# Second gate half moved into token block 1 and computed from an exponential, block sums moved behind two dots, second norm's rows in a buffer of their own

## The chip, the cores and the metric

The kernel runs on one core of a Trainium2 chip. The metric is the device time of one execution in microseconds (us). The version before takes 1873.3 us, the median of three runs (1871.72 to 1873.37).

## The reference, cut to what matters

Two decoder layers over 256 tokens of width 1024, float32. Each layer is a token mixer (attention, pooling, gated DeltaNet) with a first LayerNorm, and then the stage that this change touches:

```python
def peer_ffn(h, w_q, sub_k1, sub_k2, u_tab, v_tab):
    ...                      # 8 heads; per token and head the 16 best of 128*128 experts: idx, wts
    def block(args):         # two blocks of 128 tokens
        xb, ib, wb = args
        u_sel = u_tab[ib]
        act = jax.nn.gelu(jnp.einsum('thkd,td->thk', u_sel, xb), approximate=False)
        return jnp.einsum('thk,thkd->td', act * wb, v_tab[ib])
...
ffn = peer_ffn(h, peer_wq[i], peer_k1[i], peer_k2[i], peer_u[i], peer_v[i])
ple = jax.nn.sigmoid(h @ ple_gate[i]) * (p[i] @ ple_proj[i])
h = layer_norm(DEEPNORM_ALPHA * h + ffn + ple, ln2_g[i], ln2_b[i])
```

The `u` row and the `v` row of an expert lie side by side in HBM, 1024 floats each, so one expert is 8 KB.

## The kernel before, in words

**The stage of the experts.** Each layer treats its 256 tokens as two blocks of 128. Within a block, 8 heads times 16 ranks give 128 steps. Step n fetches for each of the 128 tokens its expert of that rank: an indirect DMA of 128 rows of 8 KB, 1 MB, issued by GpSimd (L680 in block 0, L698 in block 1) into slot n mod 8 of a ring of 8 slots. When it has landed, VectorE multiplies the first half with the tokens' rows of `h` and sums (the dot: L1722, in block 1 L1752). ScalarE makes the GELU, the weight and a 128x128 diagonal matrix of it (L1319 to L1323, in block 1 L1343 to L1349). TensorE multiplies the diagonal with the second half of the slot and adds into the PSUM tile `acc` (L912, in block 1 L931): two halves of 512 columns. Its end frees the slot (semaphore `row_used`), and GpSimd may issue the gather of step n+8.

**What stands between the steps.** `steps()` is a hand-written list of the order. VectorE chooses, in small pieces behind the dots, the experts of a later head (`select_head`). TensorE also makes the later heads' scores and, in block 0, the embedding's two products: `pp` (from the projection) and `pg` (the gate, `h @ ple_gate`), each for column halves c = 0, 1 and token blocks b = 0, 1. The gate's 4 MB of weights come in 8 pieces; `("pgw", c, j)` multiplies piece j of half c for both blocks, 8 matmuls (L799). `rows_later` lets ScalarE treat the finished gate one row later than TensorE, and VectorE two rows later. ScalarE applies the sigmoid (L1479), VectorE multiplies with the projection and adds alpha*h into `base` (L1957, L1958).

**Between the blocks.** `acc` holds one block's sum. Behind block 0's last dot VectorE waits for TensorE's last product, adds `acc` to `base` of block 0 (L1705), and TensorE then writes `base` of block 1 into `acc` by an identity product (L924) and goes on with block 1. Block 0 is unrolled in the program. In block 1 the first 6 (VectorE, ScalarE), 7 (TensorE) or 8 (GpSimd) heads are a loop on the chip.

**The norm's rows.** The gains and shifts of a LayerNorm, 1 MB when spread over the partitions, are loaded by GpSimd into `lnr`: for the first norm at L668, for the second at L671, when block 0 and 1 of the first norm are done; that is just ahead of the stage's first gather, on the same queue.

## Time and profile before

| | |
|---|---|
| median of 3 runs | 1873.3 us |
| profiled execution | 1873.84 us, span 1872.0 us |
| gathers (L680, L698) | 512, 536.9 MB of the 660.6 MB moved |
| TensorE busy | 1696.2 us, 91% |
| VectorE busy | 1371.0 us, 73% |
| ScalarE busy | 904.6 us, 48% |
| mean granted TensorE clock | 0.995 |

The span falls in four parts: the dense part of layer 0 (about 0 to 287 us), its experts (to about 931 us), and the same for layer 1 (to about 1215 and 1861 us), then the last norm and the output. Busy shares are averages over parts with different limits. In the slices of the page each place stands for 46.8 us.

### The profile page before, as it was taken

To read this page: it belongs to the slowest core of one execution; us is meant where nothing else is said; L and a number is where in the kernel's file an instruction comes from. 1 tells how busy PE (TensorE), PEld (TensorE's weight loads), DVE (VectorE), ACT (ScalarE), POOL (GpSimd) and SP (SyncE) were. 2 spreads that over 40 slices of the span, in tenths; PEclk is the share of its full clock that TensorE was granted. 3 is DMA by queue.
4 is the path that set the end of the run, shared out by engine and by line. 5 is a ranking of instruction groups with operands and counts; after the bars stand their busy time and mean duration, and the time that the engine had idled before them with its cause. 6 is when DMAs were issued, how large, how long until landed. Compare 5 with 4: busy or idle time off the path is not lost.

```text
span 1872.0 us, 26665 instructions
## 1 busy us (share of the span) xinstructions
PE 1696.2 (91%) x7454; PEld 976.1 (52%) x7454; DVE 1371.0 (73%) x3499; ACT 904.6 (48%) x2247; POOL 683.2 (36%) x585
## 2 busy tenths in 40 slices
PE   8999999999999787777799999999999998887876
PEld 8977886544444232222289778865443432222222
DVE  5987768877777777776568976787777777777754
ACT  5566534544445444444455674345444454444443
POOL 0110004544444455555311100045443555555553
PEclk9999999999999999999999999999999999999999
DMA  6644779999999999999955357799999999999997
GB/s 251 191 125 150 257 248 407 416 427 427 426 427 417 426 425 428 427 428 428 408 184 168 119 191 247 275 415 420 426 427 427 423 402 413 427 427 428 428 427 304
DMA packets 106730, 660.63 MB, mean 353 GB/s; under 512 B 11888, under 2 KB 12288, under 8 KB 40064
## 3 DMA queue, kind: packets, MB, share of 16 engines
q0 software_dynamic: 75376, 546.57, 69.8%
q1 hardware_dynamic: 31248, 112.74, 17.8%
q8 instruction: 54, 0.88, 0.2%
q14 instruction: 52, 0.43, 0.1%
HBM read 658.20 MB, written 1.06 MB: 352 GB/s over the span
## 4 chain that ended last, share of the span: by engine, by line
PE 53%; DMA 25%; issue 9%; DVE 6%; ACT 5%; POOL 1%; DVEq 1%; POOLq 0%; ACTq 0%
PE acc L912 14%; DMA arena<-experts_dram,stage 10%; DMA arena<-experts_dram,idxu 9%; PE psum L736 6%; PE psum L737 6%; PE psum L738 6%; DMA cst<-experts_dram,stage 5%; PE acc L931 4%; PE psum L767 4%; PE psum L799 2%; PE acc L736 2%; DVE arena L1722 1%; PE acc L738 1%; PE acc L737 1%; PE psum L826 1%
## 5 line engine op out<-in xcount | busy, mean ns | idle before, releaser
L931 PE MATMUL acc<-arena 128*128 128x512 f32 x896 | 440.2, 619 | 118.8 <-ACT arena L1349 118.5
L912 PE MATMUL acc<-arena 128*128 128x512 f32 x896 | 412.2, 601 | 23.9 <-ACT arena L1323 23.7
L1752 DVE CUSTOM_DVE_ANT_0 arena<-arena,h 128x1024 f32<-128x1024 f32 x224 | 274.9, 1227 | 140.8 <-DMA arena<-experts_dram,stage 60.1
L698 POOL DMA_INDIRECT arena<-experts_dram,stage x224 | 295.2, 1318 | 226.9 <-PE acc L931 173.4
L931 PEld LDWEIGHTS acc<-arena 128*128 128x128 f32 x896 | 156.9, 192 | 400.5 <-issue 400.3
L1722 DVE CUSTOM_DVE_ANT_0 arena<-arena,h 128x1024 f32<-128x1024 f32 x224 | 274.5, 1226 | 117.4 <-DMA arena<-experts_dram,idxu 113.8
L680 POOL DMA_INDIRECT arena<-experts_dram,idxu x224 | 247.6, 1105 | 300.3 <-PE acc L912 268.3
L912 PEld LDWEIGHTS acc<-arena 128*128 128x128 f32 x896 | 163.0, 189 | 251.5 <-issue 152.1
L1601 DVE TENSOR_TENSOR raw_r<-raw,w_hi_r 128x1024 fp32r<-128x1024 f32 x150 | 177.8, 1220 | 59.5 <-ACT w_hi_r L1229 58.6
L1343 ACT ACTIVATE gel<-dots 128x1 f32<-128x1 f32 x256 | 51.9, 203 | 294.5 <-DVE dots L1752 293.6
L1229 ACT ACTIVATE w_hi_r<-raw 128x1024 fp32r<-128x1024 f32 x152 | 154.2, 1054 | 50.9 <-DMA raw<-weights_dram 50.8
L1319 ACT ACTIVATE gel<-dots 128x1 f32<-128x1 f32 x256 | 51.3, 200 | 234.5 <-DVE dots L1722 233.6
L1349 ACT ACTIVATE arena<-cst,gw 128x128 f32<-128x128 f32 x256 | 102.8, 401 | 41.7 <-ACT gw L1346 16.9
L1323 ACT ACTIVATE arena<-cst,gw 128x128 f32<-128x128 f32 x256 | 102.8, 401 | 8.4
L736 PE MATMUL psum<-w_hi_r,hidden_r 128*128 128x512 f32 x256 | 101.2, 395 | 2.9 <-DVE raw_r L1601 1.9
L737 PE MATMUL psum<-raw_r,hidden_r 128*128 128x512 f32 x256 | 99.8, 390 | 0.0
L738 PE MATMUL psum<-w_hi_r,hidden_r 128*128 128x512 f32 x256 | 99.8, 390 | 0.0
L736 PE MATMUL psum<-hidden_r,w_hi_r 128*128 128x256 f32 x320 | 91.4, 286 | 0.0
L738 PE MATMUL psum<-hidden_r,raw_r 128*128 128x256 f32 x320 | 90.5, 283 | 0.0
L737 PE MATMUL psum<-hidden_r,w_hi_r 128*128 128x256 f32 x320 | 90.5, 283 | 0.0
L1346 ACT ACTIVATE gw<-gel,wst 128x1 f32<-128x1 f32 x256 | 75.4, 294 | 24.6 <-ACT gel L1343 1.7
L671 POOL DMA_DIRECT2D lnr<-lnrows_dram x2 | 1.1, 538 | 225.4 <-DVE h L1594 225.4
(294 smaller groups left out, 2702.6 us busy)
## 6 DMA issues: line engine op xcount, KB each, us to landing
raw<-weights_dram SPq DMA_DIRECT2D x168, 512.0 KB, 3.7
arena<-weights_dram SPq DMA_DIRECT2D x20, 512.0 KB, 4.6
w_hi<-weights_dram SPq DMA_DIRECT2D x12, 512.0 KB, 5.8
lnr<-lnrows_dram POOLq DMA_DIRECT2D x4, 1024.0 KB, 8.0
arena<-experts_dram,idxu POOLq DMA_INDIRECT x224, 13.2
arena<-experts_dram,stage POOLq DMA_INDIRECT x224, 13.7
lnr<-cum_dram POOLq DMA_DIRECT2D x2, 1024.0 KB, 9.1
cst<-weights_dram SPq DMA_DIRECT2D x4, 512.0 KB, 4.0
```

The lines of the kernel that those rows point to most:

```text
L680: nc.gpsimd.indirect_dma_start(slots[n % RING][:, :], None, experts[:, :], bass.IndirectOffsetOnAxis(idxu[:, n:n + 1], 0)).then_inc(slot_i ...
L698: nc.gpsimd.indirect_dma_start(slots[i % RING][:, :], None, experts[:, :], bass.IndirectOffsetOnAxis(stage[:, i:i + 1], 0)).then_inc(slot_ ...
L736: mm(dst, left[0], right[0], start=start, stop=False)
L737: mm(dst, left[0], right[1], start=False, stop=False)
L738: return mm(dst, left[1], right[0], start=False, stop=stop)
L912: last = mm(acc[:, c * 512:(c + 1) * 512], diag[:, i % 4, :], slots[n % RING][:, D + c * 512:D + (c + 1) * 512], start=n == 0, stop=n == R ...
L931: last = mm(acc[:, c * 512:(c + 1) * 512], diag[:, i % 4, :], slots[i % RING][:, D + c * 512:D + (c + 1) * 512], start=False, stop=ends)
L1229: AC(w_hi[:, n % HIS, :], raw[:, raw_slot(L, piece), :], ACT.Copy).then_inc(w_hi_ready, 1)
L1323: AC(diag[:, i % 4, :], ident, ACT.Copy, scale=gw[:, i:i + 1]).then_inc(diag_ready, 1)
L1601: TT(w_lo[:, s, :], raw[:, s, :], w_hi[:, n % HIS, :].bitcast(F32), ALU.subtract).then_inc(w_lo_ready, 1)
L1722: nc.vector.tensor_tensor_reduce(slot[:, 0:D], slot[:, 0:D], h[:, 0, :], 1.0, 0.0, ALU.mult, ALU.add, dots[:, i:i + 1]).then_inc(dot_ready, 1)
L1752: nc.vector.tensor_tensor_reduce(slots[i % RING][:, 0:D], slots[i % RING][:, 0:D], h[:, b, :], 1.0, 0.0, ALU.mult, ALU.add, dots[:, i:i + ...
```

## The change

The diff has six edits.

- The gate's half c = 1 leaves block 0: its weight pieces are multiplied by TensorE behind four steps of block 1 (`GATE_AT`: head 0 steps 4 and 10, head 1 steps 0 and 6), ScalarE drains it behind head 1 step 12, VectorE finishes it behind head 1 step 14. Half 0's four pieces stand further apart, and are finished at head 7.
- The sigmoid is made in two parts: ScalarE writes exp(-x), and VectorE adds 1 and takes the reciprocal (`gate_in`).
- Block 0's sums (`block_sums`) stand behind the second dot of block 1. Their upper half goes to `first_sums`, a free piece of `hidden`, until the gate's upper half is done. TensorE writes only the lower half of `base` of block 1 ahead of block 1's products, and the upper half at head 7.
- The first two heads of block 1 are unrolled on TensorE, ScalarE and VectorE (`OPENING = 2`).
- The second norm's rows go to `lnr2`, loaded in the dense part, behind the loads of `cdiag` and `ckeys`.
- GpSimd's descriptor scratch is 8192 bytes of a partition where the default is 16384, which makes room for `lnr2`.

```diff
-    beside |= {at: [("pgw", 0, j)] for j, at in enumerate(((5, 7), (5, 12), (5, 15), (6, 4)))}
-    beside |= {at: [("pgw", 1, j)] for j, at in enumerate(((6, 6), (6, 9), (6, 12), (7, 4)))}
-    beside |= {(6 + c, 5): [("pg", c, 0), ("pg", c, 1)] for c in range(2)}
+    beside |= {at: [("pgw", 0, j)] for j, at in enumerate(((5, 7), (5, 13), (6, 5), (6, 11)))}
+    beside |= {(7, 11): [("pg", 0, 0), ("pg", 0, 1)]}
...
+OPENING = 2
+GATE_AT = ((0, 4), (0, 10), (1, 0), (1, 6))
+GATE_OUT, GATE_IN = 12, 14
...
                         pool.dma_start(ckeys, every.broadcast_to([P, FH, T])).then_inc(ckeys_in, 16)
+                        pool.dma_start(lnr2[:, :], lnrows[L, 1]).then_inc(ln2_in, 16)
...
-                    if step == ("select", 0):
-                        pool.wait_ge(h1_ready, NB * (L + 1))
-                        pool.dma_start(lnr[:, :], lnrows[L, 1]).then_inc(ln_in, 16)
...
-                        pe.wait_ge(base_ready, L * NB + 2)
-                        for c in range(2):
-                            mm(acc[:, c * 512:(c + 1) * 512], ident, base[:, 1, c * 512:(c + 1) * 512], start=True, stop=False)
+                        pe.wait_ge(base_ready, 4 * L + 2)
+                        mm(acc[:, 0:512], ident, base[:, 1, 0:512], start=True, stop=False)
...
+                        for r in range(OPENING):
                             for i in range(TOPK):
-                                weigh(r, i, False)
+                                weigh(r, n0, i, begins=r + i == 0)
+                                if (r, i) in GATE_AT:
+                                    gate_quarter(L, 1, GATE_AT.index((r, i)))
...
+            def gate_out(L, c, b):
+
+                act.wait_ge(*filled(L, ("pg", c, b)))
+                AC(emb_gate[:, b, c * 512:(c + 1) * 512], bank(L, ("pg", c, b)), ACT.Exp, scale=-1.0).then_inc(drained(L, ("pg", c, b))[0], 1)
...
+            def block_sums(L):
+
+                dve.wait_ge(acc_filled, L * NB + 1)
+                dve.wait_ge(base_ready, 4 * L + 1)
+                TT(base[:, 0, 0:512], base[:, 0, 0:512], acc[:, 0:512], ALU.add)
+                STT(first_sums, h[:, 0, 512:D], ALPHA, acc[:, 512:D], ALU.mult, ALU.add).then_inc(acc_drained, 1)
+
+            def gate_in(L, c, b):
+
+                cs = slice(c * 512, (c + 1) * 512)
+                dve.wait_ge(*drained(L, ("pg", c, b)))
+                dve.wait_ge(*drained(L, ("pp", c, b)))
+                link(TS(emb_gate[:, b, cs], emb_gate[:, b, cs], 1.0, None, ALU.add))
+                link(nc.vector.reciprocal(emb_gate[:, b, cs], emb_gate[:, b, cs]))
+                link(TT(base[:, b, cs], base[:, b, cs], emb_gate[:, b, cs], ALU.mult))
...
+                    made = STT(base[:, b, cs], h[:, b, cs], ALPHA, base[:, b, cs], ALU.mult, ALU.add)
+                made.then_inc(base_ready, 1)
...
-                        dve.wait_ge(acc_filled, L * NB + 1)
-                        dve.wait_ge(base_ready, L * NB + 1)
-                        for c in range(2):
-                            cs = slice(c * 512, (c + 1) * 512)
-                            last = TT(base[:, 0, cs], base[:, 0, cs], acc[:, cs], ALU.add)
-                        last.then_inc(acc_drained, 1)
-                        dve.wait_ge(acc_drained, L + 1)
...
+                                if not looped and r == 0 and i == 1:
+                                    block_sums(L)
                                 next(choose, None)
+                                if not looped and r == 1 and i == GATE_IN:
+                                    for blk in range(2):
+                                        gate_in(L, 1, blk)
...
-                        turns = EH - AHEAD
+                        turns = EH - AHEAD - OPENING
+                        for r in range(OPENING):
+                            head(r, "select", False)
...
-    nc = bacc.Bacc("TRN2", target_bir_lowering=False, num_devices=1)
+    nc = bacc.Bacc("TRN2", target_bir_lowering=False, num_devices=1, dynamic_dma_scratch_size=8192)
```

How the order moves. First VectorE's program at the end of block 0 and the start of block 1, before. `ISA arena,dots<-arena,h` and `ISA cst,dots<-cst,h` are dots; the rest are pieces of the choice, and L1705 is the pair of block sums.

```order
L1510 TENSOR_REDUCE arena<-arena 128x8
L1511 TENSOR_SCALAR idxu<-arena 128x8
L1568 TENSOR_REDUCE tsum<-arena 128x1
L1569 RECIPROCAL trec<-tsum 128x1
L1570 TENSOR_SCALAR wts<-arena,trec 128x16
L1722 ISA arena,dots<-arena,h 128x1024
L1722 ISA dots 128x1
L1722 ISA cst,dots<-cst,h 128x1024
L1722 ISA dots 128x1
L1705 TENSOR_TENSOR arena<-arena,acc 128x512 x2
L1762 UNCONDITIONAL_BRANCH
```

The same place on VectorE now (the dots are L1759 in block 0 and L1792 in block 1).

```order
L1593 TENSOR_SCALAR wts<-arena,trec 128x16
L1645 TENSOR_SCALAR arena<-arena 128x512
L1646 RECIPROCAL arena<-arena 128x512
L1647 TENSOR_TENSOR arena<-arena 128x512
L1652 SCALAR_TENSOR_TENSOR arena<-h,arena 128x512
...
L1759 ISA arena,dots<-arena,h 128x1024
L1759 ISA cst,dots<-cst,h 128x1024
L1792 ISA arena,dots<-arena,h 128x1024
L1539 MAX arena<-arena 128x8 x2
L1792 ISA arena,dots<-arena,h 128x1024
L1637 TENSOR_TENSOR arena<-arena,acc 128x512
L1638 SCALAR_TENSOR_TENSOR hidden<-h,acc 128x512
```

The four instructions L1645 to L1652 stand there twice in a row, for token blocks 0 and 1, ahead of the dots of steps 14 and 15 of block 0's last head. The block sums moved from behind step 15 to behind the second dot of block 1, and the branch into the loop moved two heads further.

Second, VectorE at the end of head 1 of block 1 now; before, this was inside the loop and had the dots and the pieces of choice alone.

```order
L1593 TENSOR_SCALAR wts<-arena,trec 128x16
L1792 ISA arena,dots<-arena,h 128x1024
L1792 ISA dots 128x1
L1645 TENSOR_SCALAR arena<-arena 128x512
L1646 RECIPROCAL arena<-arena 128x512
L1647 TENSOR_TENSOR arena<-arena 128x512
L1650 TENSOR_TENSOR arena<-arena,hidden 128x512
...
L1792 ISA cst,dots<-cst,h 128x1024
L1792 ISA dots 128x1
L1809 UNCONDITIONAL_BRANCH
```

Again the gate's four instructions stand twice in a row, this time between the dots of steps 14 and 15.

Third, TensorE from block 0's end into block 1, before and then now. `psum<-raw,hidden` are gate pieces; L912 and L931, now L929 and L947, are the experts' products; L924, now L940, is the identity product.

```order
L912 MATMUL acc<-arena 128x512 x10
L799 MATMUL psum<-raw,hidden 128x512 x4
L912 MATMUL acc<-arena 128x512 x4
L912 MATMUL acc<-cst,arena 128x512 x2
L912 MATMUL acc<-arena 128x512 x14
L912 MATMUL acc<-cst,arena 128x512 x2
L924 MATMUL acc<-arena,cst 128x512 x2
L936 UNCONDITIONAL_BRANCH
```

```order
L929 MATMUL acc<-arena 128x512 x14
L929 MATMUL acc<-cst,arena 128x512 x2
L940 MATMUL acc<-arena,cst 128x512
L947 MATMUL acc<-arena 128x512 x10
L803 MATMUL psum<-raw,hidden 128x512 x4
L947 MATMUL acc<-arena 128x512 x4
L947 MATMUL acc<-cst,arena 128x512 x2
L947 MATMUL acc<-arena 128x512 x6
L803 MATMUL psum<-raw,hidden 128x512 x4
```

The identity product is one instruction instead of two, and gate pieces now stand between block 1's first products.

## Rows read from the trace of the kernel before

**Rows 1.** The page's slices, 46.8 us each: DMA busy in tenths.
```profile
DMA  6644779999999999999955357799999999999997
```
**Rows 2.** Windows: us, busy us (instructions) by engine, clock, DMA share, GB/s.
```profile
0.00:290.00 290.00, 282.30 (x2358) 243.73 (x2359) 215.44 (x380) 157.83 (x261) 18.25 (x23) 1.00 0.62 210
500.00:600.00 100.00, 98.42 (x228) 42.63 (x227) 73.57 (x214) 48.43 (x132) 43.98 (x40) 1.00 1.01 422
660.00:850.00 190.00, 150.31 (x314) 53.71 (x312) 142.03 (x427) 83.70 (x250) 110.03 (x90) 1.00 1.01 427
```
**Rows 3.** Landing times of GpSimd's transfers: L680, L698, L668 (1 MB), L710 (1 MB).
```profile
DMA to landing us min/median/max: 7.9/13.3/16.7
...
DMA to landing us min/median/max: 9.4/13.8/15.4
...
DMA to landing us min/median/max: 6.4/6.5/6.6
...
DMA to landing us min/median/max: 5.6/5.6/5.6
```
**Rows 4.** Timeline, one step of block 0: start, us, engine, line.
```profile
500.68 1.23 DVE L1722 CUSTOM_DVE_ANT_0 arena<-arena,h 128x1024 f32<-128x1024 f32 x1 [0.21 <-DMA arena<-experts_dram,idxu]
...
502.96 1.98 PE L912 MATMUL acc<-arena 128*128 128x512 f32 x4 [0.46 <-ACT arena L1323]
...
505.22 0.94 POOL L680 DMA_INDIRECT arena<-experts_dram,idxu  x1 [1.26 <-PE acc L912]
```
**Rows 5.** VectorE's groups by form: us busy, mean ns of one.
```profile
L1569 DVE RECIPROCAL trec<-tsum 128x1 f32<-128x1 f32 x32 | 5.2, 164 | 2.0
L1643 DVE RECIPROCAL beta<-spb 128x8 f32<-128x8 f32 x2 | 0.4, 203 | 0.1
L1646 DVE RECIPROCAL sp<-sp 128x24 f32<-128x24 f32 x2 | 0.6, 302 | 0.1
L1957 DVE TENSOR_TENSOR arena<-arena 128x512 f32<-128x512 f32 x8 | 5.5, 688 | 0.1
L1958 DVE SCALAR_TENSOR_TENSOR arena<-h,arena 128x512 f32<-128x512 f32 x8 | 5.5, 694 | 0.3
```
**Rows 6.** Timeline between the blocks of layer 0.
```profile
612.24 1.22 DVE L1722 CUSTOM_DVE_ANT_0 arena<-arena,h 128x1024 f32<-128x1024 f32 x1
...
614.21 1.23 DVE L1722 CUSTOM_DVE_ANT_0 cst<-cst,h 128x1024 f32<-128x1024 f32 x1 [0.74 <-DMA cst<-experts_dram,idxu]
...
619.41 1.28 DVE L1705 TENSOR_TENSOR arena<-arena,acc 128x512 f32<-128x512 f32 x2 [3.97 <-issue]
...
623.82 1.96 PE L931 MATMUL acc<-arena 128*128 128x512 f32 x4 [1.08 <-ACT arena L1349]
...
627.07 1.14 POOL L698 DMA_INDIRECT arena<-experts_dram,stage  x1 [0.77 <-POOL stage L695]
```
**Rows 7.** Timeline: second norm's load, first gather; then one window.
```profile
282.11 0.53 POOL L671 DMA_DIRECT2D lnr<-lnrows_dram  x1 [112.70 <-DVE h L1594]
287.72 1.02 POOL L680 DMA_INDIRECT arena<-experts_dram,idxu  x1 [5.07 <-DVE idxu L1511]
...
290.00:295.00 5.00, 5.00 (x25) 4.41 (x24) 3.91 (x21) 0.22 (x1) 3.77 (x5) 1.00 0.86 292
```
**Rows 8.** DMA queues of 297 to 600, and of 660 to 850.
```profile
q8 instruction: 6, 0.10, 0.1%
q14 instruction: 11, 0.09, 0.1%
...
DMA packets 11142, 81.14 MB, mean 427 GB/s; under 512 B 1238, under 2 KB 1238, under 8 KB 1238
```
**Rows 9.** Timeline: two dots of layer 1; queue q14 in 1406 to 1409.
```profile
1405.79 1.23 DVE L1722 CUSTOM_DVE_ANT_0 arena<-arena,h 128x1024 f32<-128x1024 f32 x1 [0.15 <-DVE tiu L1521]
1409.21 1.23 DVE L1722 CUSTOM_DVE_ANT_0 arena<-arena,h 128x1024 f32<-128x1024 f32 x1 [1.18 <-DMA arena<-experts_dram,idxu]
...
q14 instruction: 1, 0.01, 0.6%
```

More of the change, by code:

```diff
@@ L212 @@
 DVE_STEPS = rows_later(("pg",), 2)
+OPENED = [("pg", 1, b) for b in range(2)]
 FILLS = [s for s in STEPS if s[0] not in NO_BANK]
@@ L800, in embedding_piece, with gate_quarter @@
                 read(L, g, j, ends[1])
+            def gate_quarter(L, c, j):
+                blocks = []
+                for b in range(2):
+                    bk, use = place(L, ("pg", c, b))
+                    if j == 0:
+                        pe.wait_ge(bank_drained[bk], use)
+                    blocks.append((psum[:, bk, :], b))
+                embedding_piece(L, GROUP_OF["pg", c, 0], j, blocks)
+                if j == 3:
+                    for b in range(2):
+                        ends[b].then_inc(bank_filled[place(L, ("pg", c, b))[0]], 1)
             def turn(L, b, q):
@@ L952, in _ @@
                     if kind == "pgw":
[L953 to L963 removed]
+                        gate_quarter(L, *step[1:])
                         continue
@@ L1585, in variance, with norm @@
                 yield
-            def norm(src, r, b, n, ready, half=None):
-                link(STT(r, src, mv[:, 0:1], lnr[:, 0:D], ALU.subtract, ALU.mult))
+            def norm(src, r, b, n, ready, half=None, rows=lnr):
+                link(STT(r, src, mv[:, 0:1], rows[:, 0:D], ALU.subtract, ALU.mult))
                 yield
@@ L1690, in _ @@
                     if kind == "ln2":
-                        b = step[1]
-                        dve.wait_ge(ln_in, 16 * (2 * L + 2))
-                        if b:
+                        if step[1]:
+                            dve.wait_ge(ln2_in, 16 * (L + 1))
                             dve.wait_ge(acc_half, L + 1)
-                            for part in (statistics(acc, (acc_filled, NB * (L + 1))), norm(acc[:, :], base[:, 1, :], 1, L * 4 + 4, h2_ready, h2_half if L == DEPTH - 1 else None)):
+                            for part in (statistics(acc, (acc_filled, NB * (L + 1))), norm(acc[:, :], base[:, 1, :], 1, L * 4 + 4, h2_ready, h2_half if L == DEPTH - 1 else None, lnr2)):
                                 for _ in part:
@@ L1758, in head @@
                                 pass
-                        turns = EH - AHEAD
+                        turns = EH - AHEAD - OPENING
+                        for r in range(OPENING):
+                            head(r, "select", False)
                         n = links[0]
@@ L1767, in _ @@
                         head(EH - 1, "columns" if L + 1 < DEPTH else None, False)
+                        continue
+                    if kind == "pg":
+                        if step not in OPENED:
+                            gate_in(L, *step[1:])
                         continue
```

82 lines of the change are left out of this document (39 added, 43 removed).

## The prediction, on record before the result was known

> **What bounds the kernel now.** I read the page's slices first [rows 1]. DMA stands at 9 in two long stretches and at 3 to 7 in two others. The windows put figures on it [rows 2]: between 0 and 290 us TensorE is busy 282.30 of 290 us and the DMA share is 0.62; between 500 and 600 us the DMA share is 1.01 at 422 GB/s, and between 660 and 850 us it is 1.01 at 427 GB/s, while TensorE works 150.31 and VectorE 142.03 of the 190 us. So the dense part ends when TensorE ends, and the experts end when 256 gathers of 1,048,576 bytes have come in: at 427 GB/s that is 2.456 us for each. In the experts no engine's work counts by itself. It counts only when it leaves the DMA queues with nothing to fetch.
>
> Whether that happens follows from the ring. With 8 slots, a slot's gather of step n+8 has to land 8 x 2.456 = 19.6 us after that of step n to hold the pace. The time from landing to reissue (the turnaround) and the time from issue to landing add up to this. The landing times [rows 3] have medians of 13.3 and 13.8 us, so a usual turnaround leaves the queue full; one quiet step [rows 4] shows it whole: the dot starts at 500.68, the product at 502.96, and the gather for the same slot is issued at 505.22, some 4.5 us after the data came (the dot waited for them until just before 500.68). What a gather needs when nothing is ahead of it, m, is not shown for a gather. The nearest rows are 1 MB direct transfers, 5.6 us (L710) and 6.4 us (L668), and from above the quickest gather, 7.9 us [rows 3]. I take m = 6.4, with 5.6 and 7.9 as ends. No gather of before was under 7.9, so its queue was never empty. The queue runs dry when a turnaround exceeds 19.6 - 6.4 = 13.2 us, and the shortage is the excess.
>
> **The change part by part.** The sum is made against the profiled execution of before: 1873.84 us, of which 1872.0 is the span and 1.8 lies around it. The median of three is 1873.3.
>
> *Second norm's rows.* The load L671 stands on GpSimd's queue 5.6 us ahead of the first gather [rows 7]. It brings 1,048,576 bytes, 2.46 us at 427 GB/s, and the gathers stand behind it. Without it the first landing comes up to 2.46 us sooner in each layer, and all others with it: at most 4.9 us. At least 0: the first gather itself waits for VectorE's `idxu`, 5.07 us [rows 7], and the window from 290 to 295 us has a DMA share of only 0.86, so part of what is removed may not have been in the way. I take 4.0, less than the whole because the queue is less full there afterwards. In the dense part the megabyte goes in behind `ckeys` and `cdiag`, in a stretch with a DMA share of 0.62 where TensorE is busy 97% of the time: cost nothing, with TensorE's own work as the cover; if a weight piece behind it then comes late, at most 2.5 us a layer.
>
> *Two heads more in the program.* Instructions too come by DMA. Between 297 and 600 us, unrolled, there are 6 fetches on q8 and 11 on q14; between 660 and 850 us, in the loop, none [rows 8]. 303 us are 7.7 heads of 16 x 2.456 = 39.3 us, so 2.2 fetches a head; two more heads in two layers are 9 fetches. What one costs is bounded on one side by the rates, 424 against 427 GB/s: 0.7% of 303 us is 2.1 us over 17 fetches, 0.13 us each. On the other side is the worst place I found: two neighbouring dots of layer 1 that start 3.42 us apart, 1.18 of it waiting for the transfer, with one q14 packet between [rows 9], 0.98 us over the usual 2.44. Nine fetches: 1.2 to 8.8 us. Nearest to the mean rate I take 0.3 each, +3.
>
> *Reciprocal on VectorE.* The trace has no reciprocal of 128x512. It has 128x1 in 164 ns, 128x8 in 203 and 128x24 in 302 [rows 5]. From 8 to 24 elements the slope is 99/16 = 6.2 ns an element, and from 1 to 24 it is 6.0. For 512 elements: 302 + 488 x 6.2 = 3.33 us. The ends: 0.69 us, if it ran at the rate of the TENSOR_TENSOR of that size, and 6.4 us at twice the slope. I take 3.33, as both pairs of rows agree. `gate_in` is then a TENSOR_SCALAR (a size without a row; with one input not over the two-input 0.69 [rows 5], taken at 0.5), 3.33, 0.69 and 0.69, 5.2 us, and twice in a row with the gaps about 10.5 us. Before, the pair of a half took 2 x (0.688 + 0.694) = 2.76 us [rows 5] and stood behind a dot as well. There are four such bursts, two in each layer, and during each no dot runs.
>
> First burst, ahead of the dots of head 7's steps 14 and 15. In the trace the dot of step 14 starts at 612.24, late by some 0.6 us already because pieces of the choice came first, and step 15's starts at 614.21 on its landing [rows 6]; landings are thus at about 611.65, 614.1, then 616.55 for block 1's step 0. Shift the first by 10.5: dot 14 starts at 622.7, 11.1 us after its landing, and with the usual 4.5 its turnaround is 15.6. Dot 15 follows at 624.0, and its product ends 4.26 us later as in [rows 4] (500.68 to 502.96 + 1.98), at 628.3. The dots of block 1's steps 0 and 1 are made meanwhile. Then the sums, 1.28; TensorE, which may not touch `acc` before, starts the half identity at about 629.7, its first product of block 1 a microsecond later at 630.7, and from there to the gather's issue were 3.25 us (623.82 to 627.07 [rows 6]): 633.9. That turnaround is 633.9 - 616.55 = 17.4 us, the largest, and the shortage is 17.4 - 13.2 = 4.2 us. It includes the 2.4 of step 14, since a queue that was late once has moved all later landings. With m = 5.6 it is 3.4, with 7.9 it is 5.7.
>
> Second burst, behind the dot of step 14 of head 1 of block 1. That dot begins some 0.2 us after its landing, takes 1.3, then 10.5: the next dot starts at 12.1, and its own landing was at 2.45, so it is 9.7 late. With 5.2 us from there to reissue (a little more than in block 0; medians 13.8 and 13.3 do not differ much) the turnaround is 14.9, and the shortage 1.7 us, between 0.9 and 3.2.
>
> Per layer 5.9, both layers +11.8 us, with the ends of m 8.6 and 17.8. VectorE has only about 0.6 us a step to spare (142.03 of 190 us busy), so the backlog works off over more than a head, and pieces of the choice in it can cost another microsecond a layer.
>
> A page has another value for m. The Trainium skill ("DMA: Bandwidth & Descriptors", section "Anatomy of one DMA") gives a transfer by GpSimd about 2.0 us fixed and the bytes at 436 GB/s. That would be an m of 4.4 us, an estimate, and shortages of 2.2 us a layer, for a total near 1877; the shortest row here, 5.6 us for the same megabyte, speaks against it.
>
> *Edits at nothing.* ScalarE's Sigmoid goes, and with it changes of its table; its pieces hid behind the ring, as a DMA share of 1.01 in that stretch shows [rows 2], and what goes was not on the path. The gate's pieces leave a TensorE that is busy 98.42 of 100 us [rows 2] for one with 79%: a relief that the same ring hid before, so no gain, and no loss since 3.4 us of a piece fit into the spare time of a few steps. The block sums no longer wait where they stood: 3.97 us of VectorE's idle time [rows 6] go. The ring hid those too (no landing time came down to m), and what is late next is the sums' own wait for product 15, above. The half descriptor scratch: nothing, if several gathers still fit.
>
> Sum: -4.0 + 3.0 + 11.8 = +10.8, hence 1873.84 + 10.8 = 1884.6; against the median, 1884.
>
> **The rivals.** *A short reciprocal.* The place is the same four bursts. If the instruction takes 0.69 us, the pair takes 5.2, all turnarounds stay at 12.1 or less and nothing runs short. The point from which it decides is 2.4 us: then the boundary is short by 4.2 - 1.9 = 2.3 and the second burst by nothing, 4.6 us in all. Below it the time is within the noise: with 0.69 us, 1873.3 - 4.0 + 3.0 = 1872. For it: nothing but that the slope stands on three small sizes. Against it: those three lie on one line. A short m does the same.
>
> *The load alone.* The norm's rows give the full 4.9 us, fetches cost 0.1 each, and the bursts find cover that I do not see: 1873.3 - 4.9 + 0.9 = 1869.3. For it: medians of 13 us look ample. Against it: the arithmetic of the ring, which leaves 13.2 us.
>
> *The scratch throttles the gathers.* If 8192 bytes held the descriptors of only two gathers, the third could not be issued before the first had landed. With two in flight and 6.4 us each, a gather would take 3.2 us, 0.75 us over 2.456, times 512 = 384 us: 2257. Nothing in the trace shows the scratch; that gathers stand 13 us in the queue, some five in flight, shows only that more than two are used now. The Trainium skill ("DMA: Bandwidth & Descriptors", section "The descriptor swizzle") counts 9 + 9 descriptors per engine for a megabyte, which speaks against so small a number.
>
> *A slower reciprocal.* The price of each element may lie higher for long rows than the slope of short ones. At 4.3 us the pair is 12.4, each burst 1.9 longer, and with all four counted +7.6: 1892. The Trainium skill ("VectorE: DVE Perf Modes", sections "First, the fixed hardware budget" and "Specifications") names a repeat count of 8 for this operation and a clock of 0.96 GHz, by which an element takes 8.3 ns, an estimate. The slope of 6.2 ns disagrees.
>
> **How the numbers follow.** About 0.2% (3.7 us) is what a measurement of this kernel tells from no change: faster is below 1869.6, slower above 1877.0. The bursts' shortage as forecast 0.65, of which 0.03 ends under 1877; the short reciprocal or short m, at 1872, 0.19, of which 0.01 falls under 1869.6; the load alone 0.08; the slower reciprocal 0.06; the scratch 0.02. That makes faster 0.09, same 0.19 - 0.01 + 0.03 = 0.21, slower 0.62 + 0.06 + 0.02 = 0.70. The predicted time is 1884. The likeliest case's own range is 1878 to 1892: shortages 8.6 to 17.8, fetches 1.2 to 8.8, the load 0 to -4.9. For 8 in 10 the range takes in most of the short-reciprocal case below: 1871 to 1892.
>
> **What would show it.** The group of RECIPROCAL 128x512 near 3.3 us, 8 instances, with 10.5 us for a pair. Behind each burst dots in a row without a wait for a transfer, and TensorE waiting for VectorE; a dip of the DMA share and GB/s some 13 to 20 us later, worth 4 us at the block boundary and 2 us a head and a half later, in both layers; the least landing time of L698 near 6.4 instead of 9.4. The first gather's landing some 2 us earlier from its issue. About 9 more packets on q8 and q14. Wrong, if the DMA share stays at 1.01 through the boundary: then the ring has more cover than 13.2 us, or the reciprocal is short. Wrong in the other direction, if landings spread evenly beyond 2.456 us over a whole block.

## The result, and the profile after

The changed kernel takes 1894.9 us, the median of four runs (1893.89 to 1896.36), against 1873.31 before: a ratio of 1.0117, 95% interval 1.0105 to 1.0129. It is slower by 21.6 us, where the prediction said 10.7 and a range that ends at 1892. Its profiled execution took 1895.5 us with a span of 1893.7.

The page's slices of the kernel after (47.3 us each; clock and DMA share in tenths, then GB/s) answer to [rows 1]:

```profile
PEclk9999999999999899999999999999999999899999
DMA  7645779999999899999955357799999998999997
GB/s 250 209 124 164 246 261 396 414 427 427 427 427 427 320 427 386 428 427 427 425 194 195 118 190 245 260 426 413 426 427 426 426 428 327 419 387 427 427 427 326
```

Each layer's experts now have two dents, 320 and 386 GB/s in the first, 327 and 387 in the second (a slice with the stage's full rate has 427). The new instruction costs what was predicted, as VectorE's groups by form of the kernel after show [rows 5]:

```profile
L1646 DVE RECIPROCAL arena<-arena 128x512 f32<-128x512 f32 x8 | 26.8, 3353 | 0.3
L1645 DVE TENSOR_SCALAR arena<-arena 128x512 f32<-128x512 f32 x8 | 3.4, 421 | 0.0
```

That is 3.353 us against 3.33 from the slope. The pair of token blocks takes 10.3 us (611.83 to 622.18 below). The timeline of the kernel after at the first dent, from VectorE, TensorE and GpSimd, answers to [rows 6]:

```profile
611.83 0.42 DVE L1645 TENSOR_SCALAR arena<-arena 128x512 f32<-128x512 f32 x1
...
622.18 1.22 DVE L1759 CUSTOM_DVE_ANT_0 arena<-arena,h 128x1024 f32<-128x1024 f32 x1
...
630.88 0.69 DVE L1637 TENSOR_TENSOR arena<-arena,acc 128x512 f32<-128x512 f32 x1 [3.37 <-PE acc L929]
```

```profile
624.45 3.78 PE L929 MATMUL acc<-arena 128*128 128x512 f32 x4 [8.47 <-ACT arena L1345]
628.03 2.81 PE L929 MATMUL acc<-cst,arena 128*128 128x512 f32 x4
632.22 1.12 PE L940 MATMUL acc<-arena,cst 128*128 128x512 f32 x2 [1.38 <-DVE hidden L1638]
```

```profile
629.01 0.94 POOL L702 DMA_INDIRECT arena<-experts_dram,stage  x1 [11.11 <-PE acc L929]
...
637.07 1.82 POOL L702 DMA_INDIRECT arena<-experts_dram,stage  x1 [0.77 <-PE acc L947]
```

The dot of step 14 starts at 622.18 (forecast 622.7). But the product after it took 3.78 us where it takes 1.98 [rows 4], after TensorE had been idle for 8.47 us. The windows of the kernel after (columns as in [rows 2]) give the reason in the column ahead of the DMA share:

```profile
615.00:620.00 5.00, 0.98 (x3) 0.15 (x1) 4.90 (x5) 0.00 (x0) 1.14 (x1) 0.97 1.00 423
620.00:625.00 5.00, 0.55 (x1) 0.50 (x2) 4.93 (x8) 1.28 (x5) 0.00 (x0) 0.50 0.83 351
625.00:630.00 5.00, 5.00 (x7) 1.95 (x6) 2.33 (x6) 2.42 (x9) 0.94 (x1) 0.51 0.07 25
...
635.00:640.00 5.00, 5.00 (x13) 2.18 (x12) 4.56 (x12) 2.40 (x8) 3.53 (x3) 1.00 0.48 151
```

A window of the kernel after, cut where the clock changes, and one of the kernel before:

```profile
619.70:629.80 10.10, 5.35 (x7) 2.25 (x8) 7.56 (x13) 3.70 (x13) 0.79 (x1) 0.50 0.47 199
```

```profile
625.00:630.00 5.00, 3.63 (x8) 1.17 (x7) 3.79 (x14) 2.11 (x8) 2.44 (x3) 1.00 1.01 428
```

The granted clock falls to 0.50, the level of 1.2 GHz, within that idle stretch (at about 619.7), and the products that have to free the slots run at it until about 629.9. DMA goes to 0.07 and 25 GB/s: the queue is dry. Before, the DMA share in the same windows was 1.01 to 1.02 and the clock 1.00. The Trainium skill ("TensorE: Matmul & The Clock Gate", Part 1, "The HAM clock gate") names the lower level for a TensorE that has been idle; the rows agree. I did not carry that rule into the sum.

**An account by landings.** The profile has the time at which each gather landed. For a stretch of gathers, the excess is the time between its first and its last landing, less 2.439 us for each (the spacing of undisturbed ones). Gathers are counted from the first of a layer; the first burst stands ahead of the dot of gather 126, the second behind that of 158. Start is the first landing, in layer 1 counted from layer 0's last. In us, layer 0 / layer 1:

| kernel | start | gathers 1-60 | 60-130 | 130-147 | 147-163 | 163-180 | 180-255 |
|---|---|---|---|---|---|---|---|
| before | 297.4 / 293.3 | 2.4 / 2.8 | 5.4 / 5.8 | 1.0 / 2.4 | 0.2 / 0.2 | 0.2 / 0.2 | 2.6 / 3.1 |
| after | 293.7 / 289.9 | 6.0 / 6.0 | 4.7 / 4.7 | 9.5 / 8.5 | 0.2 / 0.5 | 4.3 / 5.1 | 2.9 / 2.8 |

The differences, both layers together, make up the 21.7 us between the spans: start -7.1, gathers 1-60 +6.7, 60-130 -1.8, the boundary (130-147) +14.6, the second burst (163-180) +8.9, the rest +0.2. Against the forecast, the two kinds of burst cost 23.5 us instead of 11.8, fetches among them.

### The profile page after: what moved, and what is told of

Its sections match the earlier page's. It is cut to its first block, busy times and chain, and to the rows that moved or that the text cites. A ratio compares the mean times of both kernels' runs of the same rounds, so it can differ in the third digit from the quotient of the medians.

```text
span 1893.7 us, 26113 instructions
## 1 busy us (share of the span) xinstructions
PE 1703.3 (90%) x7454; PEld 984.3 (52%) x7454; DVE 1397.9 (74%) x3511; ACT 893.5 (47%) x2239; POOL 676.2 (36%) x585
## 4 chain that ended last, share of the span: by engine, by line
PE 59%; DMA 20%; issue 8%; DVE 7%; ACT 4%; POOL 1%; DVEq 1%; POOLq 0%; ACTq 0%
PE acc L929 16%; DMA arena<-experts_dram,idxu 9%; PE acc L947 7%; PE psum L740 6%; PE psum L741 6%; PE psum L742 6%; DMA cst<-experts_dram,stage 5%; DMA arena<-experts_dram,stage 5%; PE psum L771 5%; PE psum L803 2%; PE acc L740 2%; DVE arena L1646 1%; PE acc L742 1%; PE acc L741 1%; PE psum L843 1%
## 5 line engine op out<-in xcount | busy, mean ns | idle before, releaser
L947 PE MATMUL acc<-arena 128*128 128x512 f32 x896 | 434.2, 619 | 89.8 <-ACT arena L1370 89.3
L929 PE MATMUL acc<-arena 128*128 128x512 f32 x896 | 421.8, 608 | 59.9 <-ACT arena L1345 59.9
L702 POOL DMA_INDIRECT arena<-experts_dram,stage x224 | 296.6, 1324 | 243.2 <-PE acc L947 154.6
L1792 DVE CUSTOM_DVE_ANT_0 arena<-arena,h 128x1024 f32<-128x1024 f32 x224 | 274.6, 1226 | 135.3 <-DMA arena<-experts_dram,stage 58.9
L1759 DVE CUSTOM_DVE_ANT_0 arena<-arena,h 128x1024 f32<-128x1024 f32 x224 | 274.5, 1226 | 124.1 <-DMA arena<-experts_dram,idxu 120.2
L947 PEld LDWEIGHTS acc<-arena 128*128 128x128 f32 x896 | 163.3, 195 | 357.0 <-issue 356.7
L929 PEld LDWEIGHTS acc<-arena 128*128 128x128 f32 x896 | 162.1, 191 | 297.7 <-ACT arena L1345 154.3
L947 PE MATMUL acc<-cst,arena 128*128 128x512 f32 x128 | 64.9, 631 | 17.4 <-ACT arena L1370 17.4
## 6 DMA issues: line engine op xcount, KB each, us to landing
lnr<-cum_dram POOLq DMA_DIRECT2D x2, 1024.0 KB, 10.1
```

Of the source, the lines that this page charges most:

```text
L702: nc.gpsimd.indirect_dma_start(slots[i % RING][:, :], None, experts[:, :], bass.IndirectOffsetOnAxis(stage[:, i:i + 1], 0)).then_inc(slot_ ...
L929: last = mm(acc[:, c * 512:(c + 1) * 512], diag[:, i % 4, :], slots[n % RING][:, D + c * 512:D + (c + 1) * 512], start=n == 0, stop=n == R ...
L947: last = mm(acc[:, c * 512:(c + 1) * 512], diag[:, i % 4, :], slots[i % RING][:, D + c * 512:D + (c + 1) * 512], start=begins and c == 1, ...
L1759: nc.vector.tensor_tensor_reduce(slot[:, 0:D], slot[:, 0:D], h[:, 0, :], 1.0, 0.0, ALU.mult, ALU.add, dots[:, i:i + 1]).then_inc(dot_ready, 1)
L1792: nc.vector.tensor_tensor_reduce(slots[i % RING][:, 0:D], slots[i % RING][:, 0:D], h[:, b, :], 1.0, 0.0, ALU.mult, ALU.add, dots[:, i:i + ...
```

## The experiments

Theory A: the loss comes from stretches of VectorE without a dot, and a part of it from TensorE's clock, which falls while TensorE waits. Rival B: the places cost by themselves (unrolled heads, the gate's pieces in block 1, the later sums), or VectorE's added work does. Each time is a median, each ratio is to the kernel before on the same chip; the ratio's 95% interval stands in brackets. The kernel before took 1872.7 to 1873.3 in every series, so times of different series are subtracted as they are. Each extract of a diff leaves out lines at `...`.

**The gate's two token blocks apart.**

```diff
-    beside |= {at: [("pgw", 0, j)] for j, at in enumerate(((5, 7), (5, 13), (6, 5), (6, 11)))}
-    beside |= {(7, 11): [("pg", 0, 0), ("pg", 0, 1)]}
+    beside |= {at: [("pgw", 0, j)] for j, at in enumerate(((5, 7), (5, 12), (5, 15), (6, 4)))}
+    beside |= {(6, 5): [("pg", 0, 0)], (6, 14): [("pg", 0, 1)]}
...
-GATE_OUT, GATE_IN = 12, 14
+GATE_OUT, GATE_IN = 7, (8, 14)
```

Half 0's four weight pieces also go back to their places of before.

> The changed kernel, with the two token blocks' halves of the gate finished apart: 5.2 us of VectorE each, eight steps from one another (half 0 behind head 6 steps 7 and, for block 1, head 7 step 0; half 1 behind head 1 steps 8 and 14), everything else as in the change. Theory A (what costs is a stretch of 10.5 us without a dot, which empties the queue and lets TensorE's granted clock fall to half): no turnaround exceeds 14 us, no clock fall, 1871 to 1876 us. Rival B (the two unrolled heads, the gate's pieces in block 1 or the sums behind two dots cost by themselves): stays above 1880.

Measured 1878.5 us, 1.0033 [1.0020, 1.0046]. 16 of the 21.6 us are gone, though not as many as A said, and the clock did fall in places (it was at 0.50 from about 621.5 to 628.4). Gathers 130-147 are back to 1.3 / 1.1; 163-180 keep 2.6 / 3.5. There the second 5.2 us came only six steps behind the first, with the backlog hardly smaller: the dot behind the first was 5.3 us late, five steps later one was still 4.3 late, and the second burst made it 8.2 and the turnaround 15.8 us. That is over the 14 us of the expectation, which took each part alone.

**Without the reciprocal.**

```diff
-                AC(emb_gate[...], bank(L, ("pg", c, b)), ACT.Exp, scale=-1.0)
+                AC(emb_gate[...], bank(L, ("pg", c, b)), ACT.Sigmoid)
-                link(TS(emb_gate[:, b, cs], emb_gate[:, b, cs], 1.0, None, ALU.add))
-                link(nc.vector.reciprocal(emb_gate[:, b, cs], emb_gate[:, b, cs]))
```

> The changed kernel with ScalarE's Sigmoid again and without the added 1 and the reciprocal; places and everything else as in the change. The two blocks' halves together then take 2.8 us of VectorE instead of 10.5. Theory A: 1871 to 1876 us, the landing times of block 1 back over 8 us. Rival B (the places, not the reciprocal): above 1880. If both have a share: between.

Measured 1874.8 us, 1.0010 [1.0001, 1.0019], as A said. Rival B's first half falls: all the other edits together cost 2 us, and the exponential with its reciprocal 1894.9 - 1874.8 = 20.1. The windows of this kernel at the two places show what is left:

```profile
620.00:650.00 30.00, 28.62 (x66) 12.38 (x65) 23.33 (x73) 10.80 (x37) 17.88 (x16) 0.99 0.94 362
700.00:735.00 35.00, 28.95 (x62) 11.19 (x61) 25.63 (x79) 14.75 (x43) 19.82 (x18) 0.96 1.01 426
```

The same windows of the kernel after:

```profile
620.00:650.00 30.00, 24.17 (x50) 10.44 (x51) 23.97 (x71) 10.75 (x37) 12.81 (x9) 0.84 0.69 260
700.00:735.00 35.00, 26.92 (x49) 11.00 (x49) 30.80 (x75) 12.66 (x41) 14.91 (x14) 0.80 0.93 372
```

The clock falls in the Sigmoid version too, a little ahead of each place, within gaps of 4.22 and 4.38 us in TensorE's work:

```profile
613.80:620.50 6.70, 5.43 (x7) 2.34 (x8) 5.58 (x11) 3.94 (x14) 0.87 (x1) 0.50 1.00 422
695.70:702.40 6.70, 5.85 (x7) 2.53 (x8) 5.67 (x16) 3.88 (x15) 1.14 (x1) 0.50 1.02 430
```

There the DMA share stays at 1.00 and 1.02, and no turnaround of that stretch exceeds 13.2 us: here the ring covered the halved clock.

**One burst alone.** The diff shows the changed lines' ends and shortens the calls.

```diff
-bank(L, ("pg", c, b)), ACT.Exp, scale=-1.0)
+bank(L, ("pg", c, b)), ACT.Sigmoid if c else ACT.Exp, scale=1.0 if c else -1.0)
+                if not c:
                     link(TS(...)); link(nc.vector.reciprocal(...))
```

> The changed kernel with the reciprocal for the gate's half 0 alone (the burst at the end of block 0); half 1 uses ScalarE's Sigmoid at its new place. If the two bursts of a layer cost apart from one another: gathers 130 to 147 as in the changed kernel (8.5 to 9.5 us over the pace), 163 to 180 as with the Sigmoid (about 1), and 1874.8 + 7.6 + 7.2 = 1889 to 1890 us. If the first burst's backlog is what made the second so dear, the rest is 8 us a layer less than the sum: below 1887.

Measured 1886.2 us, 1.0070 [1.0054, 1.0087]. The boundary's bursts cost 1886.2 - 1874.8 = 11.4 us for two layers, the second ones 1894.9 - 1886.2 = 8.7. The time lies between the two expectations (1889 and below 1887, the latter met), but gathers 130-147 at 8.4 / 8.0 and 163-180 at 0.9 / 0.7 are those of bursts that cost apart from one another: of the 2.8 us missing against 1889, 1.6 are in the size of the first burst, 0.8 us a layer less, and the rest is spread over other stretches. So the bursts cost apart from one another, and the limit of 1887 was no test of it.

**TensorE kept busy through the bursts.** In the gaps TensorE multiplies the identity with `h` into a free PSUM bank that nobody reads.

```diff
+            def keep_busy(L, b, n):
+                bk, use = place(L, ("pg", 1, 0))
+                pe.wait_ge(bank_drained[bk], use + b)
+                for _ in range(n):
+                    mm(psum[:, bk, :], ident, h[:, b, 0:512], start=True, stop=True)
...
+                        if n == RANKS - 3:
+                            keep_busy(L, 0, 18)
...
+                                if r == 1 and i in (GATE_OUT, GATE_IN):
+                                    keep_busy(L, 1, 3 if i == GATE_OUT else 14)
```

> The changed kernel with TensorE given idle products (identity times h into a free PSUM bank, never read) in the gaps of the bursts: 18 behind head 7 step 13 of block 0, 3 and 14 behind head 1 steps 12 and 14 of block 1. VectorE's bursts are unchanged. Theory A's second half (the halved clock after the burst lengthens the products that must free the slots, 3.78 us for one instead of 1.98): the clock stays at 1.00 through both places, sums start 2.7 us sooner, some 2.5 to 3 us fewer at each of four places, 1883 to 1887 us. Rival (the late products are only VectorE's lateness and the clock costs nothing on top): within 1.5 us of the changed kernel's 1895. If the added products come in the way of real ones: slower than 1895.

Measured 1909.7 us, 1.0194 [1.0179, 1.0210]: the third case of the expectation. TensorE's timeline in that kernel shows the mistake. One such product is two instructions, so that 18 of them held TensorE for 15.61 us, and the real product started at 630.56 instead of 624.45:

```profile
615.11 15.61 PE L811 MATMUL psum<-h,cst 128*128 128x512 f32 x36
630.56 1.88 PE L936 MATMUL acc<-arena 128*128 128x512 f32 x4
```

It did show that the clock stays at 1.00 and the product at 1.88 us when TensorE is not idle. With fewer:

```diff
-keep_busy(L, 0, 18)          3 if i == GATE_OUT else 14
+keep_busy(L, 0, 8)           1 if i == GATE_OUT else 6
```

> As the kernel before it with idle products in TensorE's gaps, but fewer: in that one each turned out to be two instructions and the 18 took 15.6 us where the gap is 8.5, so that real products came 6 us late. Now 8 (6.9 us) behind head 7 step 13, and 1 and 6 behind head 1 steps 12 and 14; VectorE's bursts as in the change. If the halved clock makes part of the loss: clock 1.00 through both places, the block sums start at 628.2 instead of 630.9, and each of the four places gives back 2 to 3 us: 1884 to 1888. If the clock costs nothing on top of VectorE's lateness: 1893.5 to 1896.5.

Measured 1891.0 us, 1.0096 [1.0079, 1.0113], between the two expectations. It worked at the boundary: the sums' start moved, as the identity product shows, from 632.22 to 628.96, and gathers 130-147 went from 9.5 / 8.5 to 6.4 / 5.9. At the second burst it didn't; the clock still fell, just behind the gap of 2.59 us that I had left (to 0.50 from about 711.0 to 714.4), as TensorE's timeline of this kernel shows by the product of 3.23 us:

```profile
702.58 5.31 PE L811 MATMUL psum<-h,cst 128*128 128x512 f32 x12
710.48 3.23 PE L956 MATMUL acc<-cst,arena 128*128 128x512 f32 x4 [2.59 <-ACT arena L1381]
```

So nine in both gaps:

> As e6_warm2 with 9 idle products in both gaps (there the gap left behind head 1 step 14 was 2.6 us, the clock fell to 0.66 of full speed after it and the product took 3.23 us). If a fallen clock is part of the second burst's cost too: clock 1.00 there, the product after it 1.9 us, gathers 163 to 180 at 2.5 to 3.5 us over the pace instead of 4.5 and 5.5, and 1887 to 1889. If the second burst's cost is VectorE's lateness alone: 1890.5 to 1892.

Measured 1888.1 us, 1.0083 [1.0066, 1.0100], inside what the clock theory said. TensorE's timeline and two windows of it:

```profile
702.01 7.89 PE L811 MATMUL psum<-h,cst 128*128 128x512 f32 x18
710.17 1.95 PE L956 MATMUL acc<-cst,arena 128*128 128x512 f32 x4 [0.27 <-ACT arena L1381]
```

```profile
620.00:650.00 30.00, 27.88 (x65) 11.99 (x64) 26.36 (x78) 11.80 (x40) 14.85 (x12) 1.00 0.79 310
700.00:735.00 35.00, 31.84 (x71) 12.08 (x70) 30.31 (x81) 10.91 (x37) 18.78 (x15) 1.00 0.96 384
```

With the clock at 1.00 in both windows (0.84 and 0.80 in the kernel after), and VectorE's bursts untouched, 1894.9 - 1888.1 = 6.8 us come back. That is the clock's share in these two places; by the ratios it is 6.4 us, with an interval of roughly 2.5 to 10 (an estimate from the two intervals, which don't meet). Gathers 163-180 were at 3.9 / 3.5, somewhat over the 2.5 to 3.5 that I gave.

**The load alone.** The kernel before with `lnr2` and half of the scratch, and nothing else.

```diff
+                        pool.dma_start(lnr2[:, :], lnrows[L, 1]).then_inc(ln2_in, 16)
...
-                    if step == ("select", 0):
-                        pool.wait_ge(h1_ready, NB * (L + 1))
-                        pool.dma_start(lnr[:, :], lnrows[L, 1]).then_inc(ln_in, 16)
```

> The kernel before with only the second norm's rows in their own buffer, loaded in the dense part, and half of GpSimd's scratch. The prediction's term: 4.0 us faster, 1869.3. Theory from the changed kernel's trace (the first gather lands 3.7 us sooner, but by gather 51 of layer 0 the lead is 0.0, since other limits than the queue set the pace of the first head): 1872 to 1873.5, within 0.1% of before. If the small scratch delays gathers: slower than 1876.

Measured 1873.6 us, 1.0002 [0.9993, 1.0011]: no change, as the second theory said. The prediction's 4.0 us are excluded (they would be 0.9979). The first landing did come sooner, at 293.4 and, in layer 1, 289.8 us behind layer 0's last, 7.5 us in all; gathers 1-60 then took 5.4 / 5.2 over the pace instead of 2.4 / 2.8, and gave 5.3 of it back. VectorE's timeline of the kernel before and then of this one:

```profile
297.55 1.22 DVE L1722 CUSTOM_DVE_ANT_0 arena<-arena,h 128x1024 f32<-128x1024 f32 x1 [3.29 <-DMA arena<-experts_dram,idxu]
300.00 1.23 DVE L1722 CUSTOM_DVE_ANT_0 arena<-arena,h 128x1024 f32<-128x1024 f32 x1 [1.22 <-DMA arena<-experts_dram,idxu]
```

```profile
294.14 1.21 DVE L1720 CUSTOM_DVE_ANT_0 arena<-arena,h 128x1024 f32<-128x1024 f32 x1
297.62 1.23 DVE L1720 CUSTOM_DVE_ANT_0 arena<-arena,h 128x1024 f32<-128x1024 f32 x1 [2.26 <-DMA arena<-experts_dram,idxu]
```

The first dot no longer waits for its transfer; it starts 3.4 us earlier, the second only 2.4, and by gather 80 the lead was 0.5 us in layer 0 (1.5 at gather 111 of layer 1). The same window of the kernel before and of this one, ahead of the first gather's data, shows a reason:

```profile
287.70:289.50 1.80, 1.28 (x9) 1.15 (x9) 1.70 (x11) 0.77 (x2) 1.48 (x2) 1.00 1.00 389
```

```profile
287.70:289.50 1.80, 1.28 (x9) 1.18 (x9) 1.70 (x10) 0.77 (x2) 1.50 (x2) 1.00 0.13 23
```

The load had filled DMA time that stands almost empty without it (0.13 against 1.00), because the first gather is not issued sooner (287.69 against 287.72). The landings show where the rest went. GpSimd issues the first eight gathers at the same times in both kernels (the eighth at 304.95 and 304.91), so the half scratch holds up none of them. The second gather lands 4.06 us behind the first instead of 2.46, although the DMA share is 1.03 meanwhile (293.4 to 297.5; a weight transfer of SyncE shares it): that much of the first landing's lead was none in bytes. Most of what is left goes at the eighth gather, whose issue has not moved; the share is 0.93 just ahead of its turn (307.0 to 309.7), and it lands 4.03 us behind the seventh instead of 2.44. That the median shows none of the 2.9 us by which this one profile's span is shorter is within what the runs scatter (1871 to 1875).

**The reciprocal at the old places.** The kernel before, with nothing moved.

```diff
-                        last = AC(emb_gate[...], ps, ACT.Sigmoid)
+                        last = AC(emb_gate[...], ps, ACT.Exp, scale=-1.0)
...
+                        link(TS(emb_gate[:, b, cs], emb_gate[:, b, cs], 1.0, None, ALU.add))
+                        link(nc.vector.reciprocal(emb_gate[:, b, cs], emb_gate[:, b, cs]))
```

> The kernel before with one edit: ScalarE writes exp(-x), VectorE adds 1 and takes the reciprocal, at the old places (half 0 behind head 6 step 7, half 1 behind head 7 step 7, both far from the block boundary). No load moved, nothing unrolled. By the prediction's arithmetic for a burst away from the boundary, with the m of 5.6 us that the changed kernel shows: 0.9 us for each of four, 1877. With the halved clock on top, as the changed kernel's second burst shows (4.0 to 4.9 us more in steps 163 to 180): 16 to 20 us in all, 1889 to 1893.

Measured 1896.5 us, 1.0127 [1.0110, 1.0144], 23.3 us slower: more than either expectation. Against the 20.1 us of the new places the difference is not clear of the intervals. Its windows behind the burst of head 6 in layer 0:

```profile
565.00:570.00 5.00, 1.46 (x2) 0.84 (x3) 4.86 (x14) 1.06 (x4) 0.00 (x0) 0.81 0.97 410
570.00:575.00 5.00, 5.00 (x11) 2.15 (x10) 4.79 (x20) 2.53 (x9) 0.94 (x1) 0.85 0.31 87
575.00:580.00 5.00, 5.00 (x13) 2.14 (x12) 4.69 (x11) 3.87 (x8) 1.88 (x2) 1.00 0.95 344
```

The shares 0.81 and 0.85 are means over windows in which the clock was at 0.50 for 3.4 us (568.1 to 571.5), a third of the time at the boundary above, yet the turnarounds of nine steps in a row were 15.2 to 19.3 us. VectorE was busy 4.79 of 5 us with the choice of a later head (its lag went from 10.1 us to 8.4 in six steps), and a gate piece of 3.60 us stood among TensorE's late products. So the size of the loss does not hang on the block boundary. That a burst is dear wherever the two engines have little room behind it is my reading of these rows; no run varied that room.

**More heads unrolled.** The Sigmoid version with `OPENING = 4`.

> The version with ScalarE's Sigmoid at the new places (1874.8 us), with the first four heads of block 1 unrolled instead of two. If an instruction fetch holds up one gather by about 1 us in half of the cases (the steps of 0.98 us in the changed kernel's landings beside a q14 packet), two more heads cost 1.5 to 2 us a layer: 1878 to 1879. If fetches cost 0.3 us each as the prediction took: 1877.5 at most, with 0.13 each 1876.

Measured 1878.4 us, 1.0029 [1.0018, 1.0040]: 3.6 us over the two-head version, as the first expectation said. The pages of the two-head version and of this one:

```profile
q8 instruction: 56, 0.92, 0.2%
q14 instruction: 58, 0.48, 0.1%
```

```profile
q8 instruction: 58, 0.95, 0.2%
q14 instruction: 66, 0.54, 0.1%
```

Ten fetches more, 0.36 us each on the mean; 3.3 of the 3.6 us stand in gathers 180 to 255, where the two heads are. In the landings it is not 0.36 each time: a gather with a q14 packet beside it comes either on time or about 0.97 us late.

**Eight parts behind eight dots.** Exponential and reciprocal stay, but half 1 is cut into parts of at most 1.8 us, and half 0's two token blocks stand eight steps apart as in the first experiment.

```diff
...
-GATE_AT = ((0, 4), (0, 10), (1, 0), (1, 6))
-GATE_OUT, GATE_IN = 12, 14
+GATE_AT = ((0, 1), (0, 4), (0, 7), (0, 10))
+GATE_OUT = (0, 12)
+GATE_IN = [(0, 14), (1, 1), (1, 3), (1, 5), (1, 8), (1, 10), (1, 12), (1, 14)]
...
```

> The changed kernel with exponential and reciprocal kept, but half 0's two blocks eight steps apart, and half 1 cut into eight parts of at most 1.8 us behind eight different dots, from head 0 step 14 to head 1 step 14 of block 1 (its weight pieces stand earlier for that, behind head 0 steps 1, 4, 7, 10). VectorE's total work is that of the change. If only stretches without a dot cost: as with the Sigmoid, 1874 to 1876.5. If VectorE's work itself counts (the extra 21 us of it in the kernel): over 1880. Gathers 163 to 180 should take 1 to 2 us over the pace, not 4 to 5.

Measured 1879.8 us, 1.0032 [1.0019, 1.0044]: between the two. Gathers 163-180 were at 0.2 / 1.3 as expected, but 130-147 at 5.5 / 5.6. Every dot there started within 2.6 us of its landing, so VectorE was not it; TensorE was late, with four gate pieces in ten steps. To see whether that was all (against the version just above):

```diff
+GATE_AT = ((0, 4), (0, 7), (0, 10), (0, 13))
+GATE_OUT = (0, 15)
+GATE_IN = [(1, 1), (1, 3), (1, 5), (1, 7), (1, 8), (1, 10), (1, 12), (1, 14)]
```

> As e8_spread (eight parts behind eight dots), but half 1's weight pieces stand behind head 0 steps 4, 7, 10, 13 instead of 1, 4, 7, 10 and the parts behind head 1 steps 1, 3, 5, 7, 8, 10, 12, 14. In e8_spread gathers 130 to 147 were 5.5 us over the pace, with turnarounds of 12 to 16.5 us although every dot started within 2.6 us of its landing: TensorE was late, by the pieces of 3.6 us so soon after the boundary. If so, they fall to 2 to 3.5 here and the kernel takes 1875 to 1878. If VectorE's 21 us of added work cost by themselves: it stays at 1880.

Measured 1877.5 us, 1.0027 [1.0017, 1.0036], as expected, with 1.5 / 1.5 in 130-147 where 2 to 3.5 was given. This version does all the work of the change, its reciprocals of as many elements too, and is 17 us faster than it. It is still not faster than the kernel before, and neither was any other.

## Why the prediction was right and wrong

*The mechanism was right as far as it went.* DMA bounds the experts, the ring of eight covers so much and no more, and a burst without dots empties the queue. The dents stand where they were put, in both layers.

*The reciprocal's price was right:* 3.353 us against 3.33. The rivals that lived on another price, the short one and the slower one, are out.

*The chain behind the bursts was right for a TensorE at full clock, and TensorE was not at full clock.* This is the step that failed with the larger part, 6.8 us (the other is the load's term below, 4 us): "its product ends 4.26 us later as in [rows 4]". The turnarounds in layer 0, from landing to reissue, in us:

| step | forecast | after | with TensorE kept busy |
|---|---|---|---|
| 126 | 15.6 | 17.3 | 15.5 |
| 128 | 17.4 | 20.5 | 17.8 |
| 159 | 14.9 | 16.3 | 14.6 |

With the clock held up they are the forecast to within 0.4 us. Layer 1 has the same to within 0.4 us. The halved clock added 1.7 to 2.7 us each, and 6.8 us to the kernel's time by the busy version (ratios 1.0117 and 1.0083). The prediction had even noted that no dot runs for 10.5 us and did not ask what TensorE does meanwhile.

*A dry queue costs more than its shortage.* The prediction set m at 6.4 us. The first gather of the kernel after has nothing ahead of it and shows m, 5.6 (the least landing time of L702 is 5.5; the estimate of 4.4 is out), and that should have made the cost smaller: 17.8 + 5.6 - 19.6 = 3.8 us at the boundary, 14.6 + 5.6 - 19.6 = 0.6 at the second burst. But the busy version lost 5.8 / 6.9 and 3.9 / 3.5 there, of which 1.9 / 1.3 and 0.9 / 1.1 are there in the Sigmoid version too. In its landings the gathers from the first late one on do not come at 2.44 us: at the second burst of layer 0 the late one lands 3.36 us behind its predecessor, and the next three 3.22, 3.15 and 2.74 us apart although GpSimd issued them 2.9, 2.2 and 2.0 us apart. The DMA share over those four is 0.88, 0.91, 0.95 and 1.00. Over all thirteen profiles, from a layer's tenth gather on, one issued early enough with one other ahead of it landed 3.5 us behind that one (median of 19), with two ahead 2.9 (of 96), with three or more 2.44. What limits so few gathers was not tried. Less the Sigmoid version's share, the busy version lost 3.9 / 5.6 and 3.0 / 2.4 us, against the arithmetic's 3.8 and 0.6: 0.1 to 2.4 us more each time that the queue runs dry. The two errors, m too large and no account of how slowly the queue fills again, nearly cancelled, which was luck: 11.8 forecast for the bursts, 1888.1 - 1874.8 = 13.3 measured without the clock, 20.1 with it.

*The load's term was wrong,* -4.0 us, measured +0.4 with an interval from -1.3 to +2.1. The bound "at most 2.46 us a layer" was wrong as well, since the first landing came 3.7 to 4.0 us sooner in layer 0. The load's own row in the kernel before (its landing time) shows why:

```profile
DMA to landing us min/median/max: 9.4/9.4/9.5
```

Issued at 282.11 it landed at 291.5, 3.8 us behind the first gather's issue, and the gather landed 5.9 us after it, where alone it needs 5.7. The prediction priced the load by its bytes. The step that failed was to count a lead at the start as a gain at the end. The stage's first 60 gathers are not bound by DMA alone (2.4 / 2.8 us over the pace before): the eighth is issued at the same time with and without the load, and the lead is lost there.

*The fetches were about right:* +3.0 forecast; the other edits together measured +2, and two more heads +3.6. That is 0.36 us a fetch against 0.3. The pages count 114 fetches on q8 and q14 instead of 106: 8 more, where 9 were forecast. The Trainium skill ("Runtime: NRT & Kernel Launch", "Instruction fetch mechanics") calls the cost mostly hidden. The rows differ in this place: a fetch beside full gather queues costs the gather's landing, 0.36 us on the mean.

*The edits at nothing:* the sums behind the second dot, the moved pieces of the gate and the half scratch cost nothing that can be told from the fetches; for the half scratch the load's run shows it, though not by itself (1.0002 for both together, the gathers issued at the same times, and six at most ahead of one at its issue, as before). The rival with two gathers in flight is out. The pieces are not free everywhere: put three steps apart right behind the boundary they cost 4 us a layer.

Sum of the terms as measured: load 0, fetches and the rest +2, bursts +13, clock +7, together 22, against 21.6.

*The range ended at 1892,* 3 us short. Its own ends do not give that figure: 1873.3 + 17.8 + 8.8 + 0 = 1899.9, and the prediction does not say why it stopped at 1892. A range up to 1900 would have held the result, but by luck: none of its ends held the fallen clock.

## What to carry to other kernels

When a change lets one engine run long without feeding the next, ask what every engine down the chain does meanwhile: a TensorE that idled for 8.5 us came back at half its clock and took twice as long for exactly the work that was late. A fallen clock cost time only where the work was already late: the Sigmoid version ran 6.8 us at half clock at each place and its queue stayed full. A lead or a burst is worth what the next limit leaves of it: 7.5 us at the start were worth nothing at the end, and the same reciprocals cost 20 us in four lumps and about 3 in small parts. Where a ring hides latency, keep each part of side work below what the ring has over, and leave enough steps between parts for the backlog to go.

## What the runs showed of the hardware

A RECIPROCAL on VectorE costs 6.25 ns an element between 24 (302 ns) and 512 of them (3353 ns), five times a TENSOR_TENSOR of that size (0.69 us). TensorE's granted clock fell to 0.50 within idle stretches of 8.47, 4.38 and 4.22 us, and just behind one of 2.59 us; a gap of 2.79 us ahead of 614.00 in the kernel after left it at 1.00, as did gaps of 0.27 and 0.74 us. A share between the levels, such as 0.66, is the mean of a window with both. A gather of 1 MB with an empty queue ahead landed 5.5 to 5.9 us from its issue (once 6.8). Issued early enough, it landed 3.5 us behind the one ahead of it when that was the only one (median, with 2.5 to 4.4 as ends), 2.9 with two ahead, 2.44 with three or more. An instruction fetch beside a full gather queue held up a gather by about 0.97 us or not at all.
